# The decode step's own values as one 96-row product over three head groups

## The reference, cut to what matters

```python
kv = concatenate([buf, stack([k, v], axis=2)], axis=1)      # cache rows, then the own row
g  = kv[:, cidx]                                            # 128 cached rows and the own one
s  = einsum('bthe,btjhe->bthj', q, g[:, :, :, 0])
p  = exp(s - logsumexp(s))
o  = einsum('bthj,btjhe->bthe', p, g[:, :, :, 1])           # own value: p[own] * v[own]
w  = softmax(stack(lses)); out = sum_g w[g] * o[g]          # groups combined by their denominators
kv_out = kv[:, T:]                                          # rolled caches, own row last
```

## Time and profile before

| | |
|---|---|
| median of three runs | 940.2 us (939.92 to 940.85) |
| the profiled execution, its own time | 939.62 us |
| its span, first to last instruction | 937.6 us |
| around the span | 2.0 us |
| TensorE (PE) busy | 918.5 us, 98% |
| VectorE (DVE), ScalarE (ACT), GpSimd (POOL) busy | 64%, 52%, 23% |
| mean granted TensorE clock | 0.996 |

### The profile page before, as it was taken

How to read it: one execution, slowest core, us unless ns; L and a number is a source line. 1 busy time by engine, 2 the same in 40 slices (tenths; PEclk the granted TensorE clock), 3 DMA queues, 4 the chain that set the end, 5 groups by cost and what they waited for, 6 DMA issues and landing times.

```text
span 937.6 us, 19594 instructions
## 1 busy us (share of the span) xinstructions
PE 918.5 (98%) x8007; PEld 873.2 (93%) x8007; DVE 596.2 (64%) x851; ACT 490.0 (52%) x758; POOL 219.3 (23%) x233
## 2 busy tenths in 40 slices
PE   9999999999999999989998999999999999999998
PEld 8999999999999888878898999789999999999998
DVE  6666655569965577687778653445547766666443
ACT  6444434464544766756766455336766744443342
POOL 0433330006700000068872103000001033333000
PEclk9999999999999999999999999989999999999999
DMA  9988878999888677889988687839999899998971
GB/s 356 396 301 306 306 258 304 357 379 376 311 294 278 227 270 277 281 319 363 319 301 267 226 285 249 282 126 323 350 330 339 302 337 383 337 365 298 337 230 51
DMA packets 62569, 281.17 MB, mean 300 GB/s; under 512 B 8177, under 2 KB 9329, under 8 KB 60881
## 3 DMA queue, kind: packets, MB, share of 16 engines
q10 hardware_dynamic: 39024, 131.61, 42.0%
q1 hardware_dynamic: 23456, 148.31, 41.8%
HBM read 256.64 MB, written 111.32 MB: 392 GB/s over the span
## 4 chain that ended last, share of the span: by engine, by line
PE 80%; DVE 10%; ACT 4%; issue 3%; DMA 1%; POOL 1%; SPq 0%; ACTq 0%; DVEq 0%; POOLq 0%
PE acc L410 17%; PE acc L412 16%; PE acc L411 16%; PE att L410 6%; PE att L411 6%; PE att L412 6%; DVE wl L390 2%; ACT wh L384 2%; DVE state L986 2%; PE att L800 2%; PE aux L995 1%; PE aux L1105 1%; PE att L1046 1%; PE att L1135 1%; PE att L750 1%
## 5 line engine op out<-in xcount | busy, mean ns | idle before, releaser
L390 DVE TENSOR_TENSOR wl<-raw,wh 128x1024 fp32r<-128x1024 f32 (+2 forms) x280 | 333.9, 1194 | 254.8 <-ACT wh L384 249.4
L384 ACT ACTIVATE wh<-raw 128x1024 fp32r<-128x1024 f32 (+2 forms) x280 | 277.2, 993 | 206.4 <-PE acc L412 147.2
L410 PE MATMUL acc<-hh,wh 128*128 128x264 f32 x496 | 148.1, 299 | 0.1
L412 PE MATMUL acc<-hh,wl 128*128 128x264 f32 x496 | 140.7, 284 | 0.0
L411 PE MATMUL acc<-hl,wh 128*128 128x264 f32 x496 | 140.7, 284 | 0.0
L410 PE MATMUL acc<-xh,wh 128*128 128x264 f32 x416 | 118.7, 285 | 1.1 <-DVE wl L390 1.1
L410 PE MATMUL att<-xh,wh 128*128 128x264 f32 x416 | 118.5, 285 | 0.0
L411 PE MATMUL att<-xl,wh 128*128 128x264 f32 x416 | 117.9, 283 | 0.0
L411 PE MATMUL acc<-xl,wh 128*128 128x264 f32 x416 | 117.9, 283 | 0.0
L412 PE MATMUL att<-xh,wl 128*128 128x264 f32 x416 | 117.8, 283 | 0.0
L412 PE MATMUL acc<-xh,wl 128*128 128x264 f32 x416 | 117.8, 283 | 0.0
(11 more groups left out here) (254 smaller groups left out, 1917.9 us busy)
## 6 DMA issues: line engine op xcount, KB each, us to landing
raw<-w ACTq DMA_DIRECT2D x207, 512.0 KB, 6.7
state<-state_in SPq DMA_DIRECT2D x32, 512.0 KB, 7.8
state_out<-state SPq DMA_DIRECT2D x32, 512.0 KB, 5.4
raw<-w ACTq DMA_DIRECT2D x32, 384.0 KB, 5.7
kv<-cache SPq DMA_DIRECT2D x48, 256.0 KB, 4.7
raw<-w ACTq DMA_DIRECT2D x32, 320.0 KB, 5.3
raw<-w SPq DMA_DIRECT2D x9, 512.0 KB, 8.8
kv_out<-cache SPq DMA_DIRECT2D x3, 960.0 KB, 6.7
```

The source lines that it names most:

```text
L384: nc.scalar.activation(wh[n % HI_RING][:, 0:slot_size(n)], raw[n % RAW_RING][:, 0:slot_size(n)], ACT.Copy).then_inc(hi_done, 1)
L390: nc.vector.tensor_tensor(wl[n % RAW_RING][:, 0:slot_size(n)], raw[n % RAW_RING][:, 0:slot_size(n)], wh[n % HI_RING][:, 0:slot_size(n)].bi ...
L410: nc.tensor.matmul(out, w_hi, xh, start=first, stop=False)
L412: return nc.tensor.matmul(out, w_lo, xh, start=False, stop=last)
```

## The change

The sample part of a value tile is turned together with the 24 prompt tokens ahead of it: 32 columns of `vT`, which gives 32 rows with the samples in rows 24 to 31. Group g goes to rows 32g to 32g+31 of `v_s`, so that the three groups stand below each other in 96 rows and 512 columns. `rsel` becomes 32 wide and puts the own probabilities in rows 24 to 31, zeros in the other 24; three matmuls, one for each group, write it at partitions 0, 32 and 64. `dec_own` is then 96 x 128, and one matmul for each n sums over the three groups: 4 matmuls in place of 12. Own keys move to columns of their own in `vk_s`; the two stores follow. The table of constants grows by 24 columns, which moves all that lies behind it in SBUF by 96 bytes.

```diff
-                  ("rsel", B), ("pick", B), ("own_head", AH), ("own_seq", B)):
+                  ("rsel", 32), ("pick", B), ("own_head", AH), ("own_seq", B)):
...
-    put("rsel", (row % 32 < 16)[:, None] & ((row % 16 // 8 * 4 + row % 4)[:, None] == np.arange(B)[None, :]))
+    put("rsel", (row % 32 < 16)[:, None] & (24 + (row % 16 // 8 * 4 + row % 4)[:, None] == np.arange(32)[None, :]))
...
-        vk_s = at("vk_s", 79104, [G * AW])
-        v_s, k_s = vk_s[0:B, :], vk_s[32:32 + B, :]
+        vk_s = at("vk_s", 79104, [2 * AW])
+        v_s = vk_s[0:32 * G, 0:AW]
...
-        dec_own = at("dec_own", 20000, [G, P])
+        dec_own = at("dec_own", 20000, [P])
...
-            return aux45[0:B, t % 2, S:S + P] if ph.kind == "vr" else bank5[0:B, S:S + P]
+            return aux45[0:B, t % 2, S:S + P] if ph.kind == "vr" else bank5[0:32, S:S + P]
...
-            nc.scalar.activation(small[0:B, t * P:(t + 1) * P], v_sample_rows(ph, t), ACT.Copy).then_inc(small_out, 1)
+            to = (small[0:B, t * P:(t + 1) * P] if ph.kind == "vr" else
+                  small[32 * (t // 4):32 * (t // 4) + 32, t % 4 * P:(t % 4 + 1) * P])
+            nc.scalar.activation(to, v_sample_rows(ph, t), ACT.Copy).then_inc(small_out, 1)
...
-            nc.tensor.transpose(v_sample_rows(ph, t), src[:, t % ring, S:T], ident).then_inc(turned_sem, 1)
+            first = S if ph.kind == "vr" else T - 32
+            nc.tensor.transpose(v_sample_rows(ph, t), src[:, t % ring, first:T], ident).then_inc(turned_sem, 1)
...
-            nc.tensor.matmul(att4[0:B, 0, 0:G * P], const("rsel"), dec_diag[:].rearrange("p g r -> p (g r)"),
-                             start=True, stop=True).then_inc(dec_pe, 1)
+            for g in range(G):
+                last = nc.tensor.matmul(att4[32 * g:32 * g + 32, 0, 0:P], const("rsel"), dec_diag[:, g],
+                                        start=True, stop=True)
+            last.then_inc(dec_pe, 1)
...
-            nc.scalar.activation(dec_own[0:B].rearrange("p g r -> p (g r)"), att4[0:B, 0, 0:G * P],
-                                 ACT.Copy).then_inc(dec_act, 1)
+            nc.scalar.activation(dec_own[0:32 * G], att4[0:32 * G, 0, 0:P], ACT.Copy).then_inc(dec_act, 1)
...
-            for g in range(G):
-                for n in range(4):
-                    nc.tensor.matmul(bank7[:, 256 + n * 16:256 + (n + 1) * 16],
-                                     v_s[0:B, g * AW + n * P:g * AW + (n + 1) * P], dec_own[0:B, g, 32 * n:32 * n + 16],
-                                     start=g == 0 and n == 0, stop=False, skip_group_check=True)
+            for n in range(4):
+                nc.tensor.matmul(bank7[:, 256 + n * 16:256 + (n + 1) * 16], v_s[:, n * P:(n + 1) * P],
+                                 dec_own[0:32 * G, 32 * n:32 * n + 16], start=n == 0, stop=False, skip_group_check=True)
```

More of the change, by code:

```diff
@@ L232, in trunk_step, with v_own_rows, k_own_rows @@
         v_tok = at("v_tok", 66816, [2, G * AW])
-        vk_s = at("vk_s", 79104, [G * AW])
-        v_s, k_s = vk_s[0:B, :], vk_s[32:32 + B, :]
+        vk_s = at("vk_s", 79104, [2 * AW])
+        v_s = vk_s[0:32 * G, 0:AW]
+        def v_own_rows(g):
+            return vk_s[32 * g + 24:32 * g + 32, 0:AW]
+        def k_own_rows(g):
+            return vk_s[32 * g:32 * g + B, AW:2 * AW]
         keyT = [at(f"keyT{i}", a, [AW]) for i, a in enumerate((87296, 89344, square_at - arena))]
@@ L1026, in act_samples_rows @@
             act.wait_ge(qks_psum, n + 1)
-            nc.scalar.activation(k_s[:, n * AW:(n + 1) * AW], bank6[0:B], ACT.Copy).then_inc(qks_out, 1)
+            nc.scalar.activation(k_own_rows(n), bank6[0:B], ACT.Copy).then_inc(qks_out, 1)
         def pe_scores(pe, i):
@@ L1466, in _ @@
                 w = caches[g].shape[1]
-                sp.dma_start(kv_outs[g][:, w - 1, 0:AW], k_s[0:B, g * AW:(g + 1) * AW]).then_inc(stored, 16)
-                sp.dma_start(kv_outs[g][:, w - 1, AW:2 * AW], v_s[0:B, g * AW:(g + 1) * AW]).then_inc(stored, 16)
+                sp.dma_start(kv_outs[g][:, w - 1, 0:AW], k_own_rows(g)).then_inc(stored, 16)
+                sp.dma_start(kv_outs[g][:, w - 1, AW:2 * AW], v_own_rows(g)).then_inc(stored, 16)
             for m in range(KD):
```

## The result

The changed kernel takes 935.69 us in the median of six runs (934.28 to 936.49), the one before beside it 940.06 us (939.07 to 941.49). The medians differ by 4.4 us. The ratio is 0.9949, with a 95% interval of 0.9939 to 0.9960: 0.5% faster, and the interval lies clear of no change. The profiled execution of the changed kernel took 934.28 us, with a span of 932.5 us. All lines have moved by 7 to 11: L410, L411 and L412 are now L417, L418 and L419, L1272 is L1283, L1292 is L1302, L1319 is L1328, L1105 and L1046 are L1115 and L1056, L1303 is L1312.

A forecast was written before the change was run, and what follows sets the result against it. TensorE, busy 98% of the span, was taken as the bound. Own products -1.85, clock -3.3, turn +0.1, pick -0.4 sum to -5.45 us: 934.2 from the profiled 939.62, 934.75 from the median 940.2; forecast 934.6, range 933.8 to 937.9.

The forecast's parts named there:

- The own products: At L1292, 16 of 24 records go and 8 x 0.116 us remain of 2.78: -1.85 us, at least 1.47.
- The clock, when it stays up: From the start of L1319 to the end of L1046, 8.37 us become 5.10 at full clock: up to 3.3 us back.
- the second `pe_turn`: It waits for L1085, with 1.08 us of tiles against 1.04 us: 0.1 us added, 0 to 0.2.
- That it stays up: TensorE's clock keeps full speed behind the shortened small-record stretch of 2.8 us: taken as kept, -3.3 us; open term 0 to 3.3.
- the clock falls all the same: Rival: half clock at or just behind the small records, costing 1.7 to 3.4 us; 936.3 to 938.1, named 937.2; chance 0.25.
- The pick: Own probabilities at L1272: six records of 128 columns on three column groups, side by side, replace two of 384: -0.4 us.
- The value tiles: In phase `v`, 12 transposes load 32 columns in place of 8, hidden under the matmul ahead: 0, at most 0.3 us.
- Only the records go: Rival: the clock keeps its old course and the three rsel matmuls don't overlap: 938.35 us; chance 0.07.
- the gap by switches of the array: Rival: 32-column transposes make the array change layout at each of 12 value tiles, 12 x 0.29 = 3.5 us: 941.85; chance 0.04.
- The 0.09 us: Price of the array's layout step the other way, after entering, at each value tile, within the switches rival: about 0.09 us.

The follow-up runs named there:

- before_filled_no_own: before_filled without the 12 own products (24 records), so the samples' attention output lacks their own values; 935.20 us.
- before_filled: The kernel before with 12 more dense matmuls, result unread, put into TensorE's wait for VectorE near 400 us; 941.04 us.
- after_filled: The changed kernel with 12 more dense matmuls, result unread, put into TensorE's wait for VectorE near 400 us; 936.74 us.
- after_again: The changed kernel run once more beside the others, no edit; 935.75 us.
- after_24_records: The changed kernel with 16 more records at the own products, each of the 4 products repeated twice into unread columns; 938.61 us.
- before_wide_tiles: The kernel before with the changed one's 32-column value tiles, rsel 32 wide in one matmul, still 24 own-product records; 939.69 us.
- before_spread: The kernel before with own products in three portions of 8 records ahead of tiles 1, 3 and 5, and the gather's halves apart; 944.21 us.
- after_one_pick: The changed kernel with rsel in one matmul of 384 columns and three ScalarE copies to dec_own in place of one; 935.66 us.
- before_spread_wide: As before_spread, but three tiles between own portions, six before the gather, two between its halves, VectorE's result copies one half later; 940.75 us.

## Why the prediction was right, and where it was off

**The own products.** Forecast 1.85 us less, measured 2.78 to 0.80: 1.98. That the stationary columns set the price and not the rows is borne out by 24 records of 96 rows in 2.59 us: 0.108 each, even under the 0.116 of 8 rows.

**The clock, when it stays up.** Forecast 3.3 us, less 0.1 for the second `pe_turn`. In the profiled execution gather to scores took 5.29 us for 8.37: 3.08; before_filled_no_own against before_filled gives 3.15. The wait of `pe_turn` was 0.55 for 0.33, so 0.2, the upper end.

**That it stays up.** Here the forecast's step failed in size, though the range held: "I take it as kept, -3.3". The clock stood at 1.000 over the whole span in 5 of 18 executions, the profiled one among them; with the wait near 400 us filled, four of six still show a fall, the profiled one behind the small records. The reason given was weak: the stretch "is over when the old one had still 0.9 us to go before the fall". That took the 3.7 us of small records ahead of the fall in one profile for something that the next execution keeps. In before_filled's profile small records had run for 2.9 us when the clock fell, at 620.7. In after_filled's it fell 3.4 us after the first small record (617.0 to 620.4), with 2.6 us of them and 0.8 us of other work. The rival *the clock falls all the same* had the mechanism, on dense work behind the small records and half as long, and its lower end, 936.3 us, is nearer to the five other executions (median 936.06) than my 934.6. What I missed is that it isn't one case or the other, but each in a share of the executions: a median of 935.7 lies between the two. That the forecast of 934.6 is only 1.1 us off is in part luck: the clock term of -3.3 holds for some executions and not for the median. Why the same program lets its clock fall in one execution and not in the next stays open.

**The pick.** Forecast 0.4 less, measured 0.81 to 0.42, and 0.83 when undone.

**The value tiles.** Forecast 0, measured within 0.1 us at the end of the phase; their weight load takes 0.01 us more, hidden.

**Only the records go** (938.35) didn't happen, nor did the gap by switches of the array (941.85). The 0.09 us in that rival's price stands without a row beside it.

**What I hadn't priced**: 0.27 us near 498 and 0.3 at the samples' keys, both from the order in which other engines' work falls. The 0.3 near 500 us shows in after_again and after_24_records too, but not in before_wide_tiles, which has the same value tiles; why the changed kernel has it is open. The 0.3 at the samples' keys is this one execution's: the other changed versions wait 0.2 or 0.3 us there.

The profiled execution can be added up: -1.98 - 3.08 (with the 0.2) - 0.39 + 0.27 + 0.31 = -4.9 us; the spans differ by 5.1, the other 0.2 are small shifts ahead of 600 us and in the cache wait. The medians differ by 4.4: less, since the clock fell in the five other executions, though for a shorter time than in most before.

## What to carry to other kernels

Small matmuls with 128 stationary columns cost 0.10 to 0.12 us a record here, with 8 or 16 columns streamed and with 8, 96 or 128 rows, and a stretch of them has a second price: the clock of the dense work behind. When such a stretch is shortened, work out both, and take the second as a share of executions, read from the mean clock of each one, not from one profile. Breaking the stretch into portions isn't safe: with two tiles between them it lost 4.6 us, with three it came out even, 1.0 us of it lost to a copy that was moved. And an edit that moves one engine's work can bring a wait of its own: the waits of every run are to be read, not only its clock.

## What the runs showed of the hardware that I hadn't expected

- The clock fell with TensorE at 100% busy by its records ahead of the fall (before_spread, 613.9 to 616.6) and after a wait of only 1.8 us (near 403 us), but not each time: the same wait kept 1.00 in the kernel before's profile and in after_again's.
- It stayed at half for 13.7 us while portions of small records went on, and for 3.4 us in after_filled, where dense work followed at once. Dense work doesn't always make it short: behind the cache wait of after_one_pick it was 6.8 us.
- The last load of the cache rows takes 7.0 to 9.9 us from issue to landing in programs that are nearly alike up to there, and TensorE waits up to 3.5 us for it. The clock fell behind the wait of 3.5 us and behind one of 1.8 (before_spread_wide), but not behind the other one of 1.8 (before_filled).
- The steps around a narrow transpose are the same for 8 and for 32 columns, from which I take it that the array's layout is. The Trainium skill (TensorEngine Tiling (Array Packing), Key Properties) says that a change of tiling mode drains the engine; the 0.20 us step behind both widths agrees.
